# Two rows of norm roots: spread by TensorE transposes, or through device memory

## The chip, the cores and the metric

One core of one Trainium2 chip runs the whole program. The metric is the device time of one execution in microseconds (us). Engines are called TensorE (PE in the profile, PEld for its weight loads), VectorE (DVE), ScalarE (ACT), GpSimd (POOL) and SyncE (SP); "q" behind a name is the engine's own instruction sequencer, where it issues DMAs.

## The reference, cut to what matters

Two transformer-like blocks over 512 tokens (S) of width 1024 (D) in fp32. Each begins with an RMS norm and a wide projection:

```
h = x * rsqrt(mean(x*x, axis=-1) + EPS) * g      # one root r[s] for each token s
proj = h @ w_in                                  # first block: fq fk fv fg ff px pg sq sk sv sg
z    = h @ w_in_2                                # second block: c_q, c_kv, k_rope, conv gates
```

The first block then runs forgetting attention (8 heads), a multiscale pool and stick-breaking attention (4 heads), and projects back; the second runs latent attention, a short gated convolution, a projection, a feed-forward net with its own norm, and an output gate. The root r[s] depends on the token alone, so it can be applied after the projection, to its result.

## The kernel before, in words

Tokens lie in T = 4 tiles of P = 128. `x` is transposed by TensorE into `aT` (width on the partitions) and each fp32 operand is split into a high and a low part; a product is three matmuls (`three`, L545 to L547). The norm's root is not applied to `x`: it is applied when a product leaves its PSUM bank.

There are two kinds of projection. `weights_moving` leaves tokens on the partitions, so the root is a per-partition scalar, `stat[:, 3, t]`, and ScalarE applies it while it drains the bank (fq, fv, fk, sf, and lq, lkv in the second block). `weights_still` leaves the width on the partitions and the tokens along the free dimension, so VectorE needs the roots as a row of 512 that is the same on all partitions: the tile `R` ([128, 512]). Readers of `R` are `scaled` (L1971: pg, px, fg, sg), `sqk_out` (L2131), the convolution (L2267, `c` alone, with the square of the root) and, with a third row made later, the feed-forward net (L2453).

`R` is made three times in the same way. TensorE transposes `stat[:, 3, t:t+1]` broadcast to 128x128, four times, into one bank (`R1` at L728 to L732, `R2` at L1026 to L1030, `R3` in the feed-forward net; all by `turn`, L602), and VectorE copies the bank to `R` (L2023, L2257, L2443). `R1` stands on TensorE behind fk and ahead of sf; on VectorE it stands ahead of `qk_norm(T)`, the head norm of fk. `R2` stands on TensorE behind lkv and ahead of the convolution's products; on VectorE ahead of the convolution.

The order on each engine is written out by hand; semaphores tie them together. `psum_tiles` (L79) names for each PSUM tile its bank and who drains it. SyncE does little but load weight chunks of 512 KB into two raw buffers (L399), each when the split of the chunk two before it is done; GpSimd makes the high part (L464) and the low part (L472, four pieces) in one of four slots, each when TensorE has used the chunk four before it. ScalarE issues the remaining loads from its own queue, among them `g_col2` (L1467), 1024 gains of 4 bytes each, one by one.

Of the kernel before, what the change touches and what calls it, by code (L numbers as in the profile page):

```python
# [7 lines left out]
P = 128  # L8
F32 = mybir.dt.float32
# [10 lines left out]
S, D = 512, 1024  # L20
T = S // P
# [57 lines left out]
def psum_tiles():  # L79


    tiles = {}
# [12 lines left out]
    for i in range(FOX_H // 2):  # L95
        tiles["qT", i] = (4 + i, "dve", None)
    group("fk", (0, 1, 2, 3), "act", ("fk", 3))
    tiles["R1", 0] = (7, "dve", None)
    group("sf", (4, 5, 6, 7), "act", ("sf", 2))
    n = 0  # L100
    for name in ("pg", "kT", "lfT", "px", "fg", "y", "sg"):
# [19 lines left out]
        tiles["h2_last", half] = ((7, 2)[half], "dve", None)  # L121
    group("lq", (3, 1, 4, 0), "act", ("lq", 2))
    group("lkv", (5, 6, 7, 2), "act", ("lkv", 1))
    tiles["R2", 0] = (3, "dve", None)
    n = 0
    for j in range(4):
        for i, name in enumerate(("c", "xv", "b")):
# [68 lines left out]
def hybrid_kernel(nc, x_d, w_d, cols_d, pos_d, wpool_d, pt_d, gains_d, out_d):  # L196
    tiles = tile_counts(psum_tiles())
    with ExitStack() as ctx:
        def sb(name, shape, dt=F32):
            return ctx.enter_context(nc.sbuf_tensor(name, shape, dt))  # L200

        def sem(name):
            return ctx.enter_context(nc.semaphore(name))
# [15 lines left out]
        g_col2 = sb("g_col2", [P, KD])  # L219
        g_col3 = sb("g_col3", [P, KD])  # L220
        R = sb("R", [P, S])
        PT = sb("PT", [P, 2, T, S])
        sp_sum = sb("sp_sum", [P, 2, 3, P])
        neg_tri_r = sb("neg_tri_r", [P, P], F32R)
# [45 lines left out]
        def col(name, i=0, n=1):  # L270
            return cols[:, COLS[name] + i:COLS[name] + i + n]
# [49 lines left out]
        x_back = [sem(f"x_back{t}") for t in range(T)]  # L321
        out_stored = sem("out_stored")
        masks_made, ident_made = sem("masks_made"), sem("ident_made")
        w_half, r_made, R_made = sem("w_half"), sem("r_made"), sem("R_made")
        gate_scaled, gate_made = sem("gate_scaled"), sem("gate_made")
        slot_free = sem("slot_free")
        hi_made, hi_shared, w_split, w_used = sem("hi_made"), sem("hi_shared"), sem("w_split"), sem("w_used")
# [41 lines left out]
        def full(eng, key):  # L369

            kind, n = tiles[key][1]
            eng.wait_ge(tile_full if kind == "tile" else w_used, n)

        def tbank(key):
            return bank[tiles[key][0]]
# [153 lines left out]
        def _(pe):  # L529
            mm = nc.tensor.matmul  # L530

            def bank_free(key):

                before = tiles[key][2]
                if before is not None:
                    pe.wait_ge(drained[before[0]], before[1])
# [64 lines left out]
            def turn(out, in_):  # L601
                return nc.tensor.transpose(out, in_, ident[:, :])  # L602
# [122 lines left out]

            turn_heads("qT", FOX_H // 2, P, lambda t, i: qk_raw[:, t, i * P:(i + 1) * P], qk_scaled, 1)
            weights_moving([("fk", t) for t in range(T)], group4("fk"), S)
            pe.wait_ge(r_made, 1)  # L728
            bank_free(("R1", 0))
            for t in range(T):  # L730
                last = turn(tbank(("R1", 0))[:, t * P:(t + 1) * P], stat[:, 3, t:t + 1].broadcast_to([P, P]))
            last.then_inc(tile_full, 1)  # L732
            weights_moving([("sf", t) for t in range(T)],
                           [(CH["sf"], (0, 1, 2)), (CH["sf"] + 1, (3, 4, 5)), (CH["sf"] + 2, (6, 7))], SF_W)
            for i in range(2):
# [286 lines left out]
            for n in range(3):  # L1022
                lq_step(n, T - 1)
            weights_moving([("lkv", t) for t in range(T)],
                           [(CH["lkv"], (0, 1, 2, 3)), (CH["lkv"] + 1, (4, 5, 6, 7))], RANK)
            pe.wait_ge(r_made, 2)  # L1026
            bank_free(("R2", 0))
            for t in range(T):
                last = turn(tbank(("R2", 0))[:, t * P:(t + 1) * P], stat[:, 2, 4 + t:5 + t].broadcast_to([P, P]))
            last.then_inc(tile_full, 1)  # L1030
            def turn_lats():

                pe.wait_ge(lat_scaled, 1)
# [335 lines left out]
        def _(act_):  # L1369
# [18 lines left out]
            def rsqrt(at):  # L1388

                rsq[0] += 1  # L1390
                act_.wait_ge(ms_made, rsq[0])
                own(A(stat[:, 2, at], stat[:, 1, at], ACT.Ln))
                A(stat[:, 2, at], stat[:, 2, at], ACT.Exp, scale=-0.5).then_inc(rs_made, 1)
# [47 lines left out]
            def qk_rows(name, base):  # L1441
                for t in range(T):
                    if base and t == 0:
                        act_.wait_ge(tile_full, tiles["qT", FOX_H // 2 - 1][1][1])
                    full(act_, (name, t))
                    copy(qk_raw[:, t, :], tbank((name, t))[:, :], stat[:, 3, t:t + 1]).then_inc(act_step, 1)
                    steps[0] += 1
                    n = base + t
                    if n >= 2:
                        act_.wait_ge(qk_reduced, n - 1)  # L1450
                    A(sq_tmp[:, n % 2, :], tbank((name, t))[:, :], ACT.Square, scale=stat[:, 3, t:t + 1])\
                        .then_inc(qk_squared, 1)
                    act_.wait_ge(qk_squared, n + 1)
                    order[0] += 1
                    nc.scalar.sem_inc(drained["act"], 1)

            def heads_hi(name, dst, scale, made):

                for i in range(FOX_H // 2):
                    full(act_, (name, i))  # L1460
                    for n, r in enumerate((slice(0, HD), slice(HD, P))):
                        copy(dst[r, 2 * i + n, :], tbank((name, i))[r, :], scale[r]).then_inc(made, 1)

            act_.wait_ge(const_in, 48)
            act_.wait_ge(r_made, 1)
            qk_rows("fq", 0)
            act_.dma_start(g_col2[:, :], gains_d[1, 0, :].rearrange("(k p) -> p k", p=P),  # L1467
                            allow_slow_non_contiguous=True).then_inc(g_col2_in, 16)
            rsqrt(slice(16, 48))
            for t in range(T):  # L1470
                full(act_, ("fv", t))
                drain(("fv", t), copy(fv[:, t, :], tbank(("fv", t))[:, :], stat[:, 3, t:t + 1]))
            heads_hi("qT", q_parts, col("gq"), q_hi)
            qk_rows("fk", T)
            rsqrt(slice(16, 48))
            for t in range(T):
# [187 lines left out]
            squares_x2(3)  # L1664
            rsqrt(slice(4, 8))
            act_.wait_ge(r_made, 2)
            for name, dst, w, at0 in (("lq", lat_q, LQ_W, 48), ("lkv", lat_kv, RANK, 52)):
                for t in range(T):
                    full(act_, (name, t))
                    own(copy(dst[:, t, :], tbank((name, t))[:, 0:w], stat[:, 3, 4 + t:5 + t]))  # L1670
                    drain((name, t), A(PTf[:, 3072:3072 + RANK], tbank((name, t))[:, 0:RANK], ACT.Square,
                                       scale=stat[:, 3, 4 + t:5 + t], accum_out=stat[:, 0, at0 + t:at0 + t + 1]))
            rsqrt(slice(48, 56))
            for j in range(4):
                if j == 3:
                    act_.wait_ge(w_used, CH["conv"] + 12)
                    for i in range(3):
                        split_hi(aT_hi[:, 4 + i, :], y[:, i, :], col("gc", i))
                act_.wait_ge(conv_y, j + 1)
                A(sqs[:, 1, :] if j == 0 else sq2[:, j % 2, :], y[:, j, :], ACT.Square).then_inc(sq_y, 1)  # L1680
                if j == 1:
                    for i in range(4):
                        full(act_, ("latT", i))
                        split_hi(lat_parts[:, 0, i, :], tbank(("latT", i))[:, :],
                                 col("gq2", i) if i < 2 else col("gkv2", i - 2))
                    full(act_, ("krT", 0))
                    copy(k2_high[HD:QK2, 0, :], tbank(("krT", 0))[0:ROPE, :]).then_inc(k2_rope_hi, 1)
                    act_.wait_ge(k2_rope_hi, 1)
                    copy(k2_high[HD:QK2, 1:, :], k2_high[HD:QK2, 0:1, :].bitcast(F32)
                         .broadcast_to([ROPE, MLA_H - 1, S])).then_inc(k2_rope_hi, 1)  # L1690
# [191 lines left out]
        def _(dve):  # L1882
# [9 lines left out]
            def drain(key, ins):  # L1892
                order[0] += 1
                assert tiles[key][3] == ("dve", order[0]), (key, order[0])
                ins.then_inc(drained["dve"], 1)
# [83 lines left out]
            def qk_norm(base):  # L1979
                for t in range(T):  # L1980
                    n = base + t
                    dve.wait_ge(qk_squared, n + 1)
                    V.reduce_sum(stat[:, 0, 16 + 8 * t:24 + 8 * t],
                                 sq_tmp[:, n % 2, :].rearrange("p (a b) -> p a b", b=HD), axis=AX_X)\
                        .then_inc(qk_reduced, 1)
                dve.wait_ge(qk_reduced, base + T)
                rsqrt(slice(16, 48), HD)
                v = qk_raw.rearrange("p a (b c) -> p (a b) c", c=HD)
                V.tensor_tensor(v, v, stat[:, 3, 16:48].unsqueeze(2).broadcast_to([P, T * FOX_H, HD]), ALU.mult)\
                    .then_inc(qk_scaled, 1)  # L1990
# [28 lines left out]
                    V.sem_inc(drained["dve"], 1)  # L2019

            heads_lo("qT", q_parts, q_parts, col("gq"), q_hi, q_lo)
            full(dve, ("R1", 0))
            drain(("R1", 0), V.tensor_copy(R[:, :], tbank(("R1", 0))[:, :]))  # L2023
            dve.wait_ge(drained["dve"], order[0])
            qk_norm(T)

            dve.wait_ge(drained["act"], tiles["sf", T - 1][3][1])
            v0 = lf[:, 0, :].rearrange("p (t h) -> p t h", h=FOX_H)
# [224 lines left out]
            rotate(lat_q[:, :, RANK:RANK + HALF], lat_q[:, :, RANK + HALF:LQ_W], cs[:, 0, :, :], cs[:, 1, :, :], w)  # L2253
            V.sem_inc(roped, 1)

            full(dve, ("R2", 0))
            drain(("R2", 0), V.tensor_copy(R[:, :], tbank(("R2", 0))[:, :]))  # L2257
            dve.wait_ge(drained["dve"], order[0])
            own(V.memset(u[:, :, 0:KERNEL - 1], 0.0))

            def conv_lo(j):
# [349 lines left out]
```

## Time and profile before

| | |
|---|---|
| median of 3 runs | 897.89 us (897.72 to 897.96) |
| the profiled execution | 898.09 us |
| its span in the profile | 896.4 us |
| VectorE, ScalarE, GpSimd busy | 403.0, 342.9, 500.5 us |
| granted TensorE clock | 1.00 over the span |
| moved by DMA | 86.25 MB, 96 GB/s mean |

The span runs from the first to the last instruction of the profiled execution; 1.7 us of that execution's time lie outside it. A matmul's end is modelled: the starts of two in a row tell more than a duration.

### The profile page before, as it was taken

Reading aid. Unit: us, or ns where it says so; the run is one execution under the profiler, and the core shown is the slowest. Engines: PE = TensorE matmul, PEld = TensorE weight load, DVE = VectorE, ACT = ScalarE, POOL = GpSimd, SP = SyncE. Lnnn points to the kernel's source line nnn. Section 1 sums busy time; section 2 is a strip of 40 time slices with the busy share of each in tenths; the row PEclk is TensorE's granted clock in tenths of the full one; section 3 lists DMA queues with packets and bytes.
Section 4 is the critical chain, followed back from the end, with each engine's and each line's share of the span. In section 5 each row is a group of like instructions: output and inputs, shape, how many; then the busy total and the mean of one; then the engine's idle time right before and its main releaser. Section 6 shows DMA issues by size and latency. Waiting matters only on the chain.

```text
span 896.4 us, 12958 instructions
## 1 busy us (share of the span) xinstructions
PE 889.4 (99%) x4520; PEld 734.5 (82%) x4520; DVE 403.0 (45%) x699; ACT 342.9 (38%) x693; POOL 500.5 (56%) x523
## 2 busy tenths in 40 slices
PE   9999999999999999999999999999999999999998
PEld 7889887777779888887779888888888888888887
DVE  2763485678642643876667511111111112223672
ACT  4333403567725130566648532222222223233421
POOL 6988785331475877843336564444444445555453
PEclk9999999999999999999999999999999999999999
DMA  6342362212222322221213332233322322223213
GB/s 219 96 139 81 109 167 100 66 60 82 72 81 71 132 95 90 79 87 48 69 51 99 113 117 94 94 102 103 100 94 94 118 94 94 95 99 108 71 51 118
DMA packets 29725, 86.25 MB, mean 96 GB/s; under 512 B 5224, under 2 KB 8192, under 8 KB 29680
## 3 DMA queue, kind: packets, MB, share of 16 engines
q1 hardware_dynamic: 24528, 78.65, 26.3%
q10 hardware_dynamic: 5152, 6.99, 2.9%
q8 instruction: 29, 0.48, 0.2%
q14 instruction: 16, 0.13, 0.1%
HBM read 80.93 MB, written 2.10 MB: 93 GB/s over the span
## 4 chain that ended last, share of the span: by engine, by line
PE 97%; DVE 1%; POOL 1%; ACT 0%; issue 0%; POOLq 0%; ACTq 0%; DVEq 0%
PE bank L545 28%; PE bank L547 28%; PE bank L546 28%; PE bank L602 5%; PE bank L790 2%; PE bank L893 1%; POOL w_lo L472 1%; PE bank L1135 1%; PE bank L1136 1%; PE bank L885 1%; PE bank L1134 1%; PE bank L922 1%; PE bank L857 0%; PE bank L769 0%; PE bank L854 0%
## 5 line engine op out<-in xcount | busy, mean ns | idle before, releaser
L472 POOL TENSOR_TENSOR w_lo<-raw,w_hi 128x256 fp32r<-128x256 f32 (+1 forms) x420 | 409.0, 1002 | 205.6 <-ACT w_hi L1386 199.8
L545 PE MATMUL bank<-aT_hi,w_hi 128*128 128x512 f32 (+1 forms) x584 | 225.8, 387 | 0.0
L547 PE MATMUL bank<-aT_hi,w_lo 128*128 128x512 f32 (+1 forms) x584 | 222.4, 381 | 0.0
L546 PE MATMUL bank<-aT_lo,w_hi 128*128 128x512 f32 (+1 forms) x584 | 222.2, 380 | 0.0
L545 PE MATMUL bank<-w_hi,aT_hi 128*128 128x512 f32 (+3 forms) x576 | 218.5, 379 | 0.8 <-POOL w_lo L472 0.4
L547 PE MATMUL bank<-w_hi,aT_lo 128*128 128x512 f32 (+3 forms) x576 | 213.1, 370 | 0.0
L546 PE MATMUL bank<-w_lo,aT_hi 128*128 128x512 f32 (+3 forms) x576 | 212.9, 370 | 0.0
L464 POOL TENSOR_SCALAR w_hi<-raw 128x1024 fp32r<-128x1024 f32 x70 | 76.0, 1086 | 168.1 <-PE bank L547 135.6
L1386 ACT ACTIVATE w_hi<-raw 128x1024 fp32r<-128x1024 f32 x70 | 74.1, 1060 | 231.1 <-PE bank L547 214.9
L547 PEld LDWEIGHTS bank<-aT_hi,w_lo 128*128 128x128 f32 x584 | 109.8, 188 | 21.2
L545 PEld LDWEIGHTS bank<-aT_hi,w_hi 128*128 128x128 f32 x584 | 110.0, 188 | 19.9 <-issue 0.2
L546 PEld LDWEIGHTS bank<-aT_lo,w_hi 128*128 128x128 f32 x584 | 110.0, 188 | 19.6 <-issue 0.2
L545 PEld LDWEIGHTS bank<-w_hi,aT_hi 128*128 128x128 f32 x576 | 108.5, 188 | 20.0 <-issue 2.5
L547 PEld LDWEIGHTS bank<-w_hi,aT_lo 128*128 128x128 f32 x576 | 108.3, 188 | 18.5
L546 PEld LDWEIGHTS bank<-w_lo,aT_hi 128*128 128x128 f32 x576 | 108.6, 188 | 16.0
L2467 DVE TENSOR_TENSOR aT_lo<-arena,aT_hi 128x512 fp32r<-128x512 f32 x22 | 27.3, 1250 | 78.0 <-ACT aT_hi L1386 78.0
L2456 DVE TENSOR_TENSOR arena<-arena,bank 128x512 f32 (+1 forms) x22 | 15.1, 688 | 92.8 <-PE bank L547 89.8
L2453 DVE TENSOR_TENSOR arena<-bank,R 128x512 f32<-128x512 f32 x22 | 15.2, 691 | 88.3 <-PE bank L547 87.8
L1535 ACT ACTIVATE h<-bank,negmax 128x128 f32<-128x128 f32 (+1 forms) x64 | 33.9, 530 | 29.3 <-DVE negmax L2095 28.7
L2095 DVE TENSOR_REDUCE negmax<-bank 128x1 f32<-128x128 f32 (+1 forms) x64 | 31.2, 488 | 27.1 <-PE bank L769 24.9
L1386 ACT ACTIVATE arena<-bank,stat 128x512 f32<-128x512 f32 (+3 forms) x32 | 19.6, 611 | 46.2 <-PE bank L547 43.1
L1386 ACT ACTIVATE PT<-bank 128x128 f32<-128x128 f32 (+1 forms) x64 | 27.7, 436 | 12.8 <-PE bank L602 11.8
(247 smaller groups left out, 916.3 us busy)
## 6 DMA issues: line engine op xcount, KB each, us to landing
raw<-in_weights SPq DMA_DIRECT2D x141, 512.0 KB, 3.3
x<-in_x ACTq DMA_DIRECT2D x4, 512.0 KB, 5.3
y_out<-x SPq DMA_DIRECT2D x7, 256.0 KB, 4.1
x<-in_x SPq DMA_DIRECT2D x3, 512.0 KB, 8.5
g_post<-in_gains ACTq DMA_DIRECT2D x3, 512.0 KB, 3.4
k_twice<-k_twice ACTq DMA_DIRECT2D x2, 512.0 KB, 5.5
x<-in_x SPq DMA_DIRECT2D x2, 256.0 KB, 3.5
raw<-in_weights SPq DMA_DIRECT2D x2, 256.0 KB, 4.6
```

Source lines behind the costliest of these rows:

```text
L464: nc.gpsimd.tensor_scalar(w_hi[:, s, :], raw[:, r, :], 1.0, 1.0, ALU.mult, ALU.mult).then_inc(hi_made, 1)
L472: lo = nc.gpsimd.tensor_tensor(w_lo[:, s, at], raw[:, r, at], w_hi[:, s, at].bitcast(F32), ALU.subtract)
L545: mm(out, st_hi, mv_hi, start=start, stop=False)
L546: mm(out, st_hi, mv_lo, start=False, stop=False)
L547: return mm(out, st_lo, mv_hi, start=False, stop=stop)
L602: return nc.tensor.transpose(out, in_, ident[:, :])
L790: last = mm(bank[6][r0:r0 + HD, kb * P:S], v_[:, kb, i * HD:(i + 1) * HD], pt_of[i % 2][:, kb, kb * P:S], start=(kb == 0), stop=(kb == T - 1),
L1386: return A(out, in_, ACT.Copy, scale=scale)
L1535: A(P_buf[:, n % 4, 0:kw], bank[n % 3][:, 0:kw], ACT.Exp, bias=negmax[:, n % 8:n % 8 + 1], accum_out=esum[:, n % 8:n % 8 + 1]).then_inc(ex ...
L2095: V.tensor_reduce(negmax[:, n % 8:n % 8 + 1], bank[n % 3][:, 0:kw], AX_X, ALU.max, negate=True)\
L2453: V.tensor_tensor(sg_t[:, slot, :], bank[2 * slot][:, :], R[:, :], ALU.mult).then_inc(ffn_scaled, 1)
L2467: V.tensor_tensor(aT_lo[:, slot, :].unsqueeze(1), act[:, bass.ds(k, 1), :], aT_hi[:, slot, :].bitcast(F32).unsqueeze(1), ALU.subtract).the ...
```

## The change

The transposes, the two PSUM tiles `R1` and `R2` and VectorE's two copies go away; `R3` stays. In their place ScalarE issues two DMAs for each row. `roots_to_row` writes the 512 roots from `stat` ([128 partitions, 4]) to a row in device memory, each as an element of 4 bytes. `row_to_all` waits for that write and reads the row back to all 128 partitions of `R` (128 runs of 2 KB, 256 KB). VectorE waits for `R_in`.

For the first row, `roots_to_row(0)` stands ahead of the draining of fq, `row_to_all(0)` behind the high parts of q and ahead of the draining of fk; VectorE waits behind `qk_norm(T)`. For the second, `roots_to_row(1)` stands ahead of the draining of lq, `row_to_all(1)` behind the draining of lkv and its rsqrt; VectorE waits ahead of the convolution.

```diff
 psum_tiles:
-    tiles["R1", 0] = (7, "dve", None)
-    tiles["R2", 0] = (3, "dve", None)
 hybrid_kernel:
+        r_rows = nc.dram_tensor("r_rows", (2, S), F32).ap()
-        w_half, r_made, R_made = sem("w_half"), sem("r_made"), sem("R_made")
+        w_half, r_made = sem("w_half"), sem("r_made")
+        r_row_out, R_in = sem("r_row_out"), sem("R_in")
 TensorE:
             weights_moving([("fk", t) for t in range(T)], group4("fk"), S)
-            pe.wait_ge(r_made, 1)
-            bank_free(("R1", 0))
-            for t in range(T):
-                last = turn(tbank(("R1", 0))[:, t * P:(t + 1) * P], stat[:, 3, t:t + 1].broadcast_to([P, P]))
-            last.then_inc(tile_full, 1)
             weights_moving([("sf", t) for t in range(T)],
...
-            pe.wait_ge(r_made, 2)
-            bank_free(("R2", 0))
-            for t in range(T):
-                last = turn(tbank(("R2", 0))[:, t * P:(t + 1) * P], stat[:, 2, 4 + t:5 + t].broadcast_to([P, P]))
-            last.then_inc(tile_full, 1)
 ScalarE:
+            def roots_to_row(n, of):
+
+                act_.dma_start(r_rows[n, :].rearrange("(t p) -> p t", p=P), of, allow_slow_non_contiguous=True)\
+                    .then_inc(r_row_out, 16)
+
+            def row_to_all(n):
+
+                act_.wait_ge(r_row_out, n * 16 + 16)
+                act_.dma_start(R[:, :], r_rows[n:n + 1, :].broadcast_to([P, S])).then_inc(R_in, 16)
+
             act_.wait_ge(const_in, 48)
             act_.wait_ge(r_made, 1)
+            roots_to_row(0, stat[:, 3, 0:T])
             qk_rows("fq", 0)
...
             heads_hi("qT", q_parts, col("gq"), q_hi)
+            row_to_all(0)
             qk_rows("fk", T)
...
             rsqrt(slice(4, 8))
             act_.wait_ge(r_made, 2)
+            roots_to_row(1, stat[:, 2, 4:4 + T])
             for name, dst, w, at0 in (("lq", lat_q, LQ_W, 48), ("lkv", lat_kv, RANK, 52)):
...
             rsqrt(slice(48, 56))
+            row_to_all(1)
             for j in range(4):
 VectorE:
             heads_lo("qT", q_parts, q_parts, col("gq"), q_hi, q_lo)
-            full(dve, ("R1", 0))
-            drain(("R1", 0), V.tensor_copy(R[:, :], tbank(("R1", 0))[:, :]))
-            dve.wait_ge(drained["dve"], order[0])
             qk_norm(T)
+            dve.wait_ge(R_in, 16)
...
-            full(dve, ("R2", 0))
-            drain(("R2", 0), V.tensor_copy(R[:, :], tbank(("R2", 0))[:, :]))
-            dve.wait_ge(drained["dve"], order[0])
+            dve.wait_ge(R_in, 32)
             own(V.memset(u[:, :, 0:KERNEL - 1], 0.0))
```

## Rows read from the trace of the kernel before

**Rows 1.** The page, part 1: busy us, share of the span, instructions.
```profile
PE 889.4 (99%) x4520; PEld 734.5 (82%) x4520; DVE 403.0 (45%) x699; ACT 342.9 (38%) x693; POOL 500.5 (56%) x523
```
**Rows 2.** The page, part 4: the chain that ended last, by engine.
```profile
PE 97%; DVE 1%; POOL 1%; ACT 0%; issue 0%; POOLq 0%; ACTq 0%; DVEq 0%
```
**Rows 3.** Waits of PE: who for whom, us in total, times, longest.
```profile
PE bank L545 <- POOL w_lo L472: 0.4, 1, 0.4
```
**Rows 4.** The chain in order of time: start us, us, piece.
```profile
53.30 1.75 PE bank L602 x16
...
76.84 0.44 PE bank L602 x4
77.27 0.12 PE bank L545
...
294.76 0.44 PE bank L602 x4
295.20 0.23 PE bank L545
```
**Rows 5.** Timeline of PE around R2: start us, us, engine, line, operation.
```profile
294.61 0.60 PE L602 MATMUL bank<-ident,stat 128*128 128x128 f32 x4
...
294.96 0.47 PE L545 MATMUL bank<-aT_hi,w_hi 128*128 128x512 f32 x1
...
295.27 0.39 PE L546 MATMUL bank<-aT_lo,w_hi 128*128 128x512 f32 x1
```
**Rows 6.** Timeline of ACT, first block: the same columns, idle before in brackets.
```profile
27.79 0.69 ACT L1386 ACTIVATE arena<-bank,stat 128x512 f32<-128x512 f32 x1 [1.60 <-DVEq L1964]
...
33.33 0.39 ACTq L1467 DMA_DIRECT2D g_col<-in_gains  x1
...
49.25 0.69 ACT L1386 ACTIVATE arena<-bank,stat 128x512 f32<-128x512 f32 x1 [14.40 <-PE bank L547]
...
53.92 5.63 ACT L1386 ACTIVATE q_parts<-bank,cols 64x512 fp32r<-64x512 f32 x8
72.86 0.69 ACT L1386 ACTIVATE arena<-bank,stat 128x512 f32<-128x512 f32 x1 [13.30 <-PE bank L547]
```
**Rows 7.** Timeline of ACT around lkv.
```profile
290.49 0.47 ACT L1386 ACTIVATE arena<-bank,stat 128x256 f32<-128x256 f32 x1 [6.09 <-PE bank L547]
...
296.81 0.21 ACT L1393 ACTIVATE stat<-stat 128x8 f32<-128x8 f32 x1
```
**Rows 8.** Line L1467 (g_col2), its last line: issue to landing.
```profile
DMA to landing us min/median/max: 2.3/2.3/2.3
```
**Rows 9.** Line L1517: ns of an issue, min/median/max.
```profile
L1517 ACTq DMA_DIRECT2D k_low<-c_parts x8: 580/854/2067, 115.1 to 124.8; - x8
```
**Rows 10.** Busy time by stretch; the last two columns: DMA share, GB/s.
```profile
28.00:30.00 2.00, 2.00 (x10) 1.67 (x9) 0.69 (x1) 1.88 (x4) 2.00 (x4) 1.00 0.00 0
...
34.00:36.00 2.00, 2.00 (x11) 1.65 (x10) 1.37 (x4) 0.46 (x2) 1.81 (x3) 1.00 0.71 39
```
**Rows 11.** Timeline of SP: the load of the seventh chunk (c = 6).
```profile
30.54 0.33 SPq L399 DMA_DIRECT2D raw<-in_weights  x1
```
**Rows 12.** The page, part 6: KB each, median us to landing.
```profile
raw<-in_weights SPq DMA_DIRECT2D x141, 512.0 KB, 3.3
...
k_twice<-k_twice ACTq DMA_DIRECT2D x2, 512.0 KB, 5.5
```
**Rows 13.** Timeline of POOL: the two parts of that chunk.
```profile
34.40 1.05 POOL L464 TENSOR_SCALAR w_hi<-raw 128x1024 fp32r<-128x1024 f32 x1
35.53 4.92 POOL L472 TENSOR_TENSOR w_lo<-raw,w_hi 128x256 fp32r<-128x256 f32 x4
```
**Rows 14.** Timeline of DVE, both blocks.
```profile
77.31 0.69 DVE L2023 COPY R<-bank 128x512 f32<-128x512 f32 x1 [14.91 <-PE bank L602]
...
307.64 0.69 DVE L2257 COPY R<-bank 128x512 f32<-128x512 f32 x1
...
317.10 0.69 DVE L2267 TENSOR_TENSOR arena<-bank,R 128x512 f32<-128x512 f32 x1 [4.19 <-PE bank L547]
```

## The prediction

> **What bounds the kernel now.** I read the page's first part, then its chain, then TensorE's waits, then the chain in order of time around the places that the change touches. TensorE is busy 889.4 us [rows 1] of a span of 896.4 and makes 97% of the chain that ended last [rows 2]. Of its waits for other engines, the only one on the weights' supply is 0.4 us, once [rows 3]. So the time is the sum of what TensorE issues. An edit gains if it takes slots out of TensorE's order, and costs if it makes another engine late enough for TensorE to stand still; work on VectorE or ScalarE is worth nothing in itself. Both groups of transposes stand in the chain: four at 76.84, 0.44 us, and four at 294.76, 0.44 us [rows 4], with matmuls directly before and behind.
>
> **The change part by part.**
>
> *TensorE loses eight transposes.* The chain books 0.44 + 0.44 = 0.88 us [rows 4]. The starts say the same in two pieces: from the first transpose, 294.61, to the next matmul, 294.96, is 0.35 us; and that matmul's successor follows after 0.31 us, where a matmul of 512 columns takes 0.23 us in the chain, 0.08 us more [rows 4, 5]. Upper end of the gain: 0.88 us. Lower end: 2 x 0.35 = 0.70 us, if the slow first matmul is due to the change of shape from 256 to 512 columns and not to the transposes. I take 0.88, since the chain's own figure holds both pieces. What stands behind each group (sf, the convolution) simply starts earlier. TensorE also loses its waits for `r_made` and for a bank, which ended long before and are worth nothing.
>
> The trace gives 0.35 us for four transposes, 0.09 us each, before the after-effect [rows 5]. The Trainium skill, "TensorE: Matmul & The Clock Gate", section "Back-to-back issue gap", puts a sustained pair of weight load and 128-column matmul at about 81 ns; by it eight would be worth an estimated 0.65 us. The trace has the duration here and decides.
>
> *VectorE loses two copies and gains two waits.* The copies are 0.69 us each [rows 14]. The first copy waited 14.91 us for TensorE's R1 and ended at 78.00, and the norm of fk stood behind it. Its first input is two ScalarE operations of 0.69 us behind 72.86 [rows 6], so the norm can start at 74.2, 3.8 us earlier, and end up to that much earlier. TensorE wants the result only at the turning of k, behind the 96 matmuls of sf at 0.12 us and the 48 of pg at 0.23 us from 77.27 on [rows 4], near 99.8, so that is worth nothing. The second copy, at 307.64, is followed by work that waits 4.19 us for TensorE at 317.10 [rows 14]: again nothing. What is late next is in both cases TensorE's own next product.
>
> *The waits for R_in.* ScalarE issues the first read behind q's high parts, 53.92 + 5.63 = 59.55 [rows 6]. The nearest rows for its landing are 3.3 us for a weight load of twice its 256 KB, and 5.5 us, the slowest 512 KB on ScalarE's queue [rows 12]; with an issue of at most 2.1 us [rows 9] R is there between 62 and 67.2. VectorE comes to its wait behind the norm of fk, so after the 77.31 of its old copy less 3.1 us [rows 14], at 74 at the very least: a margin of 7 us. The second read is issued behind 296.81 + 0.21 [rows 7] and lands between 300.7 and 304.6; VectorE reaches it at 307.6 [rows 14], 3 us of margin at the worst bound, 7 us at the likely one. The convolution is queued behind that wait, and TensorE's banks behind the convolution; I cost both waits at 0.
>
> *ScalarE gains four issues and two waits.* The nearest row for an issue is g_col2's, 0.39 us, also a scatter of 4-byte elements; the dearest is one of L1517, 2.07 us [rows 6, 9]. The first, at 27.8, delays the draining of fq by 0.4 to 2.1 us; TensorE needs that chain at the turning of q at 53.30 [rows 4], and ScalarE idles 14.40 us before its next drain at 49.25 [rows 6]. The read at 59.6 falls into 13.30 us of idleness [rows 6], and its wait asks for a write issued 32 us earlier. The third delays the draining of lq, behind which ScalarE idles 6.09 us [rows 7]; lq's banks are wanted again only by the convolution at 295.20 [rows 4]. The fourth stands ahead of nothing until the convolution's first square, 16 us later. All four: 0, cover 6 us or more against 2.1.
>
> *The DMA engines gain two writes of 512 elements and two reads of 256 KB.* The nearest row for such a write is g_col2: 1024 elements, landed 2.3 us after its issue [rows 8], and in 34 to 36 us the engines were 71% busy moving 39 GB/s [rows 10]: small elements take engine time out of proportion. Half as many should hold them for 1 to 2.3 us. Both writes fall into stretches where the DMA share was 0.00, at 28 to 30 us [rows 10] and again at 279 to 282 us (two such rows, one shown); the next weight load after the first is issued at 30.54 [rows 11]. The reads cost at most half a weight load, 1.7 us [rows 12], on a load whose chunk TensorE wants over 10 us later: from 60 us on GpSimd waits for TensorE to free a slot, so it runs three chunks of 5.4 us ahead (24 matmuls of 0.23 us, [rows 4]). Cost 0.
>
> This is where a rule speaks against the change, and its row is the 71% for small reads [rows 10]; no row before has small writes to device memory. The Trainium skill, "DMA: Bandwidth & Descriptors", section "Specifications", says that below 512 bytes the engines do a read-modify-write. If that made the writes several times as dear as g_col2's reads, it would be the slower rival below; it leaves the sum as it is.
>
> **Sum.** -0.88 + 0 + 0 + 0 + 0 = -0.88 us. From the profiled execution: 898.09 - 0.88 = 897.21 us, of which 895.5 is span. That execution lies 0.20 us above the median of the runs, so the median should come to 897.89 - 0.88 = 897.01 us.
>
> **The rivals.**
>
> *A, the writes crowd out the seventh weight chunk (slower).* Place: the load issued at 30.54 [rows 11], landing at 33.84; GpSimd takes it at 34.40 and is done at 40.45, slowed in this stretch [rows 13]. TensorE wants it at 53.30 less 48 matmuls of 0.227 us, 42.4 [rows 4]. The margins, 0.56 and 1.95 us, make 2.5. If the write holds the engines from 28.2 for W us, the load is late by W - 2.3 and TensorE stands still for W - 4.8. At W = 5.7 the gain is used up; at W = 8, three and a half times g_col2's landing, the median is 897.01 + 3.2 = 900.2 us. For it: the engine share of small elements. Against: W of at most 2.3 by the nearest row.
>
> *B, the gain is given back.* If a later stage is bound by supply and not by TensorE, an earlier start is waited away. The only such wait is 0.4 us [rows 3], and what releases it hangs on TensorE itself. Or only the lower end, 0.70, comes. Time 897.2 to 897.8 us, within the bound.
>
> *C, the freed VectorE moves more than itself (faster).* GpSimd's 4.92 us for four pieces [rows 13] shows that VectorE can slow it by 2 us; the norm of fk now lies elsewhere against GpSimd's work. If supply were what TensorE waits for, up to 2 us would be had: 895.0 us. Against: TensorE waits 0.4 us in all for that supply.
>
> *D, R lands late.* The second wait would hold VectorE past 307.6. It needs a landing of over 10 us, and then VectorE has 4.19 us of idleness to catch up [rows 14]. Price: 0 up to a landing of 14 us, 1 us per us beyond.
>
> **How the numbers follow.** A change of under 0.2% (1.8 us) is about what a measurement of this kernel can't tell from none. Forecast (-0.88, own range 896.6 to 897.4): 0.80. B: 0.10. A: 0.05. C: 0.03. D: 0.02. Within 0.2% are the forecast, B, and the small end of A and D: 0.90. Faster is C with a small rest: 0.04. Slower is most of A and D: 0.06. The range runs from 896.1 (the forecast and 0.9 us for shifts that I have not seen) to 898.3, which takes in B and the start of A; outside lie C and most of A and D.
>
> **What would show it.** Right: TensorE's instructions fall by 8, no L602 on `stat` but the third group, a span near 895.5; the ends of fk and of lkv directly followed by sf and the convolution, the second 0.44 us and the later stages 0.88 us; no wait of VectorE on `R`; fq's drain 0.4 us later; the norm of fk 2 to 4 us earlier, the turning of k 0.44. Wrong: a TensorE wait on `w_lo` between 37 and 48 us (A), a wait of VectorE at L2267 released by the read of R (D), PE waits beyond 1 us that were not there (B), or ScalarE's issues above 2.1 us.

## The result and the profile after

The changed kernel took 900.30 us (median of 10 runs, 899.01 to 902.00); the kernel before, in runs on the same chip, 897.88 us (897.45 to 898.23). The ratio is 1.0029, with a 95% interval of 1.0020 to 1.0037: slower by 2.4 us, where 0.88 us less was forecast. That is 0.3% of the time. The runs after spread over 3 us, those before over 0.8. The profiled execution was the slowest of the ten, 902.00 us, with a span of 900.2 us against 896.4.

The page after, its first line and the first lines of parts 1 and 4, against [rows 1, 2]:

```profile
span 900.2 us, 12941 instructions
...
PE 890.8 (99%) x4512; PEld 735.7 (82%) x4512; DVE 396.0 (44%) x697; ACT 342.7 (38%) x693; POOL 498.8 (55%) x523
...
PE 93%; POOL 3%; DMA 2%; DVE 1%; issue 1%; ACT 0%; SPq 0%; POOLq 0%; DVEq 0%; ACTq 0%
```

TensorE issues eight matmuls fewer, as the change says. But its share of the chain fell from 97% to 93%, and DMA is now in the chain with 2%, GpSimd with 3%. That is more than the time lost, since the chain up to the wait now runs by way of the load and GpSimd and no longer by TensorE. "Busy" hides part of that, since a matmul at the lower clock is busy for longer. TensorE's waits, after, against [rows 3]:

```profile
PE bank L545 <- POOL w_lo L472: 2.7, 2, 2.3
```

The chain in order of time says where. After, stretches of it (start us, us, piece), against [rows 4]:

```profile
30.11 10.48 DMA raw<-in_weights
...
41.20 1.05 POOL w_hi L464
...
43.03 2.10 POOL w_lo L472 x3
...
45.18 0.79 PE bank L545
...
57.91 1.75 PE bank L602 x16
103.97 2.19 PE bank L602 x20
...
331.57 2.18 PE bank L602 x20
```

The load of the seventh weight chunk, issued at 30.11, landed 10.48 us later; such a load takes 3.3 us [rows 12]. Now the transfer that stands ahead of it, ScalarE's line L1456 in the changed kernel (the write of the roots, both of them), and L1462 (the read back): ns of the issues, and us from issue to landing.

```profile
L1456 ACTq DMA_DIRECT2D r_rows<-stat x2: 388/390/391, 28.0 to 283.4; - x2
...
DMA to landing us min/median/max: 10.6/10.7/10.8
```

```profile
L1462 ACTq DMA_DIRECT2D R<-r_rows x2: 327/336/345, 60.7 to 301.3; - x2
...
DMA to landing us min/median/max: 3.2/3.5/3.7
```

The write of 2 KB takes three times as long as a load of 512 KB. GpSimd's timeline after, against [rows 13], and SP's and TensorE's side of it:

```profile
41.20 1.05 POOL L464 TENSOR_SCALAR w_hi<-raw 128x1024 fp32r<-128x1024 f32 x1 [7.34 <-DMA raw<-in_weights]
42.34 2.78 POOL L472 TENSOR_TENSOR w_lo<-raw,w_hi 128x256 fp32r<-128x256 f32 x4
```

```profile
42.50 0.39 PE L547 MATMUL bank<-w_hi,aT_lo 128*128 128x512 f32 x1
45.18 0.79 PE L545 MATMUL bank<-w_hi,aT_hi 128*128 128x512 f32 x1 [2.29 <-POOL w_lo L472]
45.77 0.63 PE L546 MATMUL bank<-w_lo,aT_hi 128*128 128x512 f32 x1
46.20 0.63 PE L547 MATMUL bank<-w_hi,aT_lo 128*128 128x512 f32 x1
...
47.90 0.63 PE L545 MATMUL bank<-w_hi,aT_hi 128*128 128x512 f32 x1
48.33 0.47 PE L546 MATMUL bank<-w_lo,aT_hi 128*128 128x512 f32 x1
48.63 0.39 PE L547 MATMUL bank<-w_hi,aT_lo 128*128 128x512 f32 x1
```

Read the starts: 2.68 us from the last matmul before the wait to the first behind it, where 0.23 is usual, so 2.45 us are lost. Then eight steps take 3.45 us (45.18 to 48.63) in place of 1.82: the granted clock had fallen to its lower level, 1.2 GHz, at the end of the time in which TensorE stood still (1.00 from 44.8 to 45.0 us, 0.68 from 45.0 to 45.2), and came back to 2.4. Busy time by stretch shows the same; the third figure from the right is the granted clock:

```profile
42.00:44.00 2.00, 0.89 (x4) 0.39 (x3) 1.52 (x2) 0.00 (x0) 1.92 (x4) 1.00 0.00 0
44.00:46.00 2.00, 0.82 (x2) 0.73 (x3) 1.51 (x2) 0.00 (x0) 2.00 (x3) 0.77 0.00 0
46.00:48.00 2.00, 2.00 (x6) 1.51 (x6) 0.80 (x1) 0.00 (x0) 1.92 (x4) 0.50 0.76 252
```

The sum closes on landmarks that both traces have. The first is a group of eight transposes of `x` on TensorE, ahead of everything that was changed: it starts at 22.31 us in the trace of before and at 22.79 after. So this execution was 0.48 us behind before the write was issued at 28.01. The turning of q came 4.61 us later (53.30 to 57.91): these 0.48, 2.45 of waiting, 1.63 of the lower clock, and 0.05 left. The next two landmarks in the chain of before are the turnings of k and of the latents:

```profile
99.81 2.18 PE bank L602 x20
...
327.87 2.18 PE bank L602 x20
```

From the turning of q to that of k at 103.97 is 46.06 us, against 46.51 before: 0.45 less, the first group of transposes. The turning of the latents at 331.57 against 327.87 is 3.70 us late where k was 4.16 late: 0.46 less, the second group. So both gains came, each at its forecast size, and 4.1 us were paid ahead of them.

### The profile page after: what moved, and what is told of

The parts are those of the page before. It is cut to its first block, busy times and chain, and to the rows that moved or that the text cites. A ratio compares the mean times of both kernels' runs of the same rounds, so it can differ in the third digit from the quotient of the medians.

```text
span 900.2 us, 12941 instructions
## 1 busy us (share of the span) xinstructions
PE 890.8 (99%) x4512; PEld 735.7 (82%) x4512; DVE 396.0 (44%) x697; ACT 342.7 (38%) x693; POOL 498.8 (55%) x523
## 4 chain that ended last, share of the span: by engine, by line
PE 93%; POOL 3%; DMA 2%; DVE 1%; issue 1%; ACT 0%; SPq 0%; POOLq 0%; DVEq 0%; ACTq 0%
PE bank L545 27%; PE bank L547 27%; PE bank L546 27%; PE bank L602 4%; DMA raw<-in_weights 2%; PE bank L785 2%; POOL w_lo L472 2%; PE bank L888 1%; PE bank L1125 1%; PE bank L1126 1%; PE bank L880 1%; PE bank L1124 1%; PE bank L917 1%; PE bank L852 0%; PE bank L764 0%
## 5 line engine op out<-in xcount | busy, mean ns | idle before, releaser
L472 POOL TENSOR_TENSOR w_lo<-raw,w_hi 128x256 fp32r<-128x256 f32 (+1 forms) x420 | 404.7, 992 | 205.8 <-ACT w_hi L1376 200.0
L464 POOL TENSOR_SCALAR w_hi<-raw 128x1024 fp32r<-128x1024 f32 x70 | 78.6, 1123 | 173.8 <-PE bank L547 131.0
```

The source lines that it names most:

```text
L464: nc.gpsimd.tensor_scalar(w_hi[:, s, :], raw[:, r, :], 1.0, 1.0, ALU.mult, ALU.mult).then_inc(hi_made, 1)
L472: lo = nc.gpsimd.tensor_tensor(w_lo[:, s, at], raw[:, r, at], w_hi[:, s, at].bitcast(F32), ALU.subtract)
```

## The experiments

The first question was which part of the change makes the wait.

**e1, the write alone.** The kernel before, and in ScalarE's order:

```diff
             act_.wait_ge(r_made, 1)
+            roots_to_row(0, stat[:, 3, 0:T])
             qk_rows("fq", 0)
...
+            act_.wait_ge(r_row_out, 16)
             qk_rows("fk", T)
```

> The kernel before, with only the first write of 512 elements of 4 bytes added ahead of the draining of fq; both groups of transposes stay and nothing reads the row. Theory W (the write holds the DMA engines, the seventh weight chunk's load waits behind it, TensorE stands still once and comes back at the lower clock): landing of the write near 10.7 us, the load issued near 30.5 us lands near 40.6, a TensorE wait of about 2.3 us on w_lo between 42 and 45 us, and a time 4 to 5 us above before (no transposes saved), about 902. Rival S (the slower time comes from the shifted work of ScalarE and VectorE or from the reads back, and the write is hidden): within 0.3 us of before, 897.9.

Measured: 903.97 us against 898.13, ratio 1.0052 (1.0037 to 1.0068). The write landed after 11.7 us, TensorE waited 3.83 us at once where 2.3 were expected, and the clock was at the lower level behind it. Against before, the write that nobody reads costs more, 5.8 us by the medians, than the whole change did; S is out. Part of the distance is that five of e1's seven runs had the lower clock and four of the changed kernel's ten (a table further down has them); e1's two others, 900.19 and 900.73, lie 2.1 and 2.6 us above before. TensorE's wait in e1, and the stretch behind it with the granted clock third from the right:

```profile
46.46 0.79 PE L547 MATMUL bank<-w_hi,aT_hi 128*128 128x512 f32 x1 [3.83 <-POOL w_lo L474]
...
46.00:48.00 2.00, 1.54 (x4) 1.25 (x5) 0.28 (x1) 0.00 (x0) 1.92 (x3) 0.54 0.19 35
```

**e2, the second row alone.** The changed kernel with its first row made as before (the lines of the diff that concern `R1` put back, `roots_to_row(0)` and `row_to_all(0)` taken out).

> The changed kernel with its first row made by the four transposes and VectorE's copy again; only the second row goes through device memory, at the changed kernel's place. Theory W: the second write falls where GpSimd is far enough ahead, TensorE does not wait, four transposes are gone: before less 0.44 us, 897.4. Rival S (each transfer costs something of its own wherever it stands): above before by 1 us or more.

Measured: 897.89 against 898.13 us, ratio 1.0003 (0.9993 to 1.0012), by the medians 0.24 us less: too small for these runs to tell from none (0.44 were expected), and 1 us more, the least that S asks, is the interval's upper end (1.0012 is 1.1 us). The trace decides: the write landed after 10.5 us, the two loads issued from 276 to 292 us after 6.6 us (median) where 3.3 are usual, TensorE's waits were those of before, the turnings of q and k stood 46.51 us apart as before and those of k and of the latents 227.60 (99.65 to 327.25) against 228.06: 0.46 less. A write of 10.5 us is free there, though it holds loads there too.

**e3, the first write later.**

```diff
-            roots_to_row(0, stat[:, 3, 0:T])
             qk_rows("fq", 0)
...
-            row_to_all(0)
+            roots_to_row(0, stat[:, 3, 0:T])
             qk_rows("fk", T)
             rsqrt(slice(16, 48))
+            row_to_all(0)
```

> The changed kernel with the first write moved 32 us later in ScalarE's order, behind the high parts of q (near 60 us), and its read behind the draining of fk and the rsqrt (near 82 us). Same transfers, another place. Theory W: at 60 us GpSimd is three chunks ahead, so a load that is 8 us late costs TensorE nothing: before less 0.88 us, 897.0, no wait on w_lo before 100 us. Rival P (a write of 10.7 us stops TensorE wherever it falls, since loads come every 4 to 5 us): 900 or more, with a wait between 65 and 90 us.

Measured: 897.52 against 898.13 us, ratio 0.9994 (0.9985 to 1.0004); its writes landed after 9.7 and 11.2 us. No wait beyond those of before; q to k 46.06 us, k to the latents 227.62: both gains. By the medians 0.6 us less than before, where 0.9 was expected, with a sign that the interval leaves open. The three loads of 56 to 70 us landed after 6.3 us (median), 3.1 in the same stretch of before: the loads are held as well, and TensorE doesn't come to wait for them. The same transfers, 29 us later (56.89 against 28.01), cost near 3 us less than in the changed kernel: P is out, the place decides.

**e4, the same place, other runs.**

```diff
-                act_.dma_start(r_rows[n, :].rearrange("(t p) -> p t", p=P), of, allow_slow_non_contiguous=True)\
+                act_.dma_start(r_rows[n, :].rearrange("(p t) -> p t", t=T), of)\
...
-                act_.dma_start(R[:, :], r_rows[n:n + 1, :].broadcast_to([P, S])).then_inc(R_in, 16)
+                act_.dma_start(landing(n), r_rows[n:n + 1, :].broadcast_to([P, S])).then_inc(R_in, 16)
...
             dve.wait_ge(R_in, 16)
+            own(V.tensor_copy(R[:, :].rearrange("p (t a) -> p t a", t=T),
+                              landing(0).rearrange("p (a t) -> p t a", t=T)))
```

> The changed kernel with both writes as 128 runs of 16 bytes in place of 512 elements of 4 (the row lies in another order in device memory, is read into a landing tile, and VectorE's copy puts it in order: two copies of about 0.7 us, which are off TensorE's path). Same bytes, a quarter of the elements, same early place. Theory N (the landing goes by the number of elements): 2 us and a quarter of the other 8.7, so near 4.2 us, the seventh chunk in time, before less 0.88 us, 897.0. Rival H (the landing goes by the trip of a write to device memory, not by the number): still near 10.7 us, and the time of the changed kernel, 900.3.

Measured: 897.28 against 898.13 us, ratio 0.9989 (0.9979 to 0.9998): 0.85 us less, what was forecast for the change itself (the interval: 0.2 to 1.9 us less). TensorE did not wait more than before. Line L1460 in e4, the write:

```profile
L1460 ACTq DMA_DIRECT2D r_rows<-stat x2: 336/338/340, 28.9 to 278.9; - x2
...
DMA to landing us min/median/max: 1.4/2.3/3.1
```

H is out: a trip to device memory is not what takes 10.7 us. But N is not shown by it, for runs of 16 bytes differ from elements of 4 in more than number. The second question was what makes the small write dear. All further kernels but the last are the kernel before with one write in e1's place.

**e5, into on-chip memory.** Four DMAs of 128 elements in place of one of 512:

```diff
+                for t in range(T):
+                    act_.dma_start(PTf[0:1, 2608 + t * P:2608 + (t + 1) * P], of[:, t:t + 1],
+                                   allow_slow_non_contiguous=True).then_inc(r_row_out, 16)
```

> The kernel before with the same 512 elements of 4 bytes written at the same place, but into one partition of on-chip memory instead of device memory (as four DMAs of 128 elements, one behind the other on ScalarE's queue); nothing reads them. Theory M (a write of a few bytes to device memory is what is dear): landing of the last under 4 us after its issue, the seventh chunk in time, the time of before, 897.9. Theory N (each small element is dear, wherever it goes): together near 10 us, a TensorE wait near 43 us, 900 to 904.

Measured: 898.22 against 897.99 us, ratio 1.0002 (0.9992 to 1.0012). The four landed 2.0 to 3.8 us after their issues, the last of these at 31.4. M holds so far, N falls: 512 small elements as such are not dear. The four DMAs of 128 differ from one of 512 in more than the memory; e6 takes that up.

**e6, 128 bytes apart.**

```diff
+        r_rows = nc.dram_tensor("r_rows", (2, S, 32), F32).ap()
...
+                act_.dma_start(r_rows[n, :, 0].rearrange("(t p) -> p t", p=P), of, allow_slow_non_contiguous=True)\
```

> The kernel before with the first write to device memory as 512 elements of 4 bytes, but 128 bytes apart, so that no two touch the same 64 bytes; nothing reads them. Theory L (elements of one stretch of 64 bytes wait for each other, since each one's surroundings are read and written back): landing near 3 us, no TensorE wait, 897.9. Theory N (a fixed cost for each small element): near 10.7 us as before, a wait of 2 to 4 us, 900 to 904.

Measured: 897.88 against 897.99 us, ratio 1.0002 (0.9992 to 1.0012). The same 512 elements in one DMA into the same memory, and e6's line L1468 says:

```profile
DMA to landing us min/median/max: 1.9/1.9/1.9
```

**e7, half of the elements,** the first 256 of the row, close together (`stat[:, 3, 0:T // 2]` into `r_rows[n, 0:S // 2]`).

> The kernel before with half of the first write: 256 elements of 4 bytes (the roots of two of the four token tiles), nothing reads them. If the landing grows with the number of elements: 2 and half of 8.7, so near 6.3 us; the load issued near 30.5 lands some 2 us late and TensorE, with 2.5 us of margin, does not wait or waits under 0.5 us: within 0.5 us of before, 897.9. If the landing has a large fixed part: near 10 us and 900 or more.

Measured: 901.28 against 897.99 us, ratio 1.0043 (1.0028 to 1.0057). This one I expected wrongly: I still took the landing to grow with the number. It took 10.6 us for 256 elements, as for 512. With e6 it says the opposite of N: 512 elements apart are cheap, 256 close together are dear. So M in its plain form is out as well: a write to device memory is not dear in itself. Line L1468 in e7, and TensorE behind its wait:

```profile
DMA to landing us min/median/max: 10.6/10.6/10.6
```

```profile
44.49 0.50 PE L547 MATMUL bank<-w_hi,aT_hi 128*128 128x512 f32 x1 [2.25 <-POOL w_lo L474]
44.83 0.40 PE L548 MATMUL bank<-w_lo,aT_hi 128*128 128x512 f32 x1
```

**e9 to e12, the distance.** As e6 with `(2, S, n)` for n of 2, 4, 8 and 16, one execution each.

> The kernel before with the first write of 512 elements of 4 bytes, 8 bytes apart in device memory; nothing reads them. Theory C (elements that lie in one block of device memory are written one after another, and the landing goes by how many share a block): 8 in 64 bytes in place of 16, so 2 us and half of 8.7, near 6.3 us. Rival T (any neighbour in the same block costs the whole): near 10.7 us.

> The same with elements 16 bytes apart. Theory C: 4 in 64 bytes, near 4.2 us, the seventh chunk in time. Rival T: near 10.7 us and a TensorE wait near 43 us.

> The same with elements 32 bytes apart. Theory C with blocks of 64 bytes: 2 in a block, near 3 us; with blocks of 32 bytes: 1.9 us, as at 128 bytes apart. Rival T with blocks of 64 bytes: near 10.7 us.

> The same with elements 64 bytes apart. With blocks of 64 bytes or less by either theory 1.9 us, as at 128 bytes apart; above 3 us only if the block is larger.

Line L1468 in e9, e10, e11 and e12, in this order:

```profile
DMA to landing us min/median/max: 5.0/5.0/5.0
```

```profile
DMA to landing us min/median/max: 3.4/3.4/3.4
```

```profile
DMA to landing us min/median/max: 1.9/1.9/1.9
```

```profile
DMA to landing us min/median/max: 1.8/1.8/1.8
```

| bytes apart | in 32 bytes | landing us | GpSimd's wait for the seventh chunk |
|---|---|---|---|
| 4 (changed kernel, two writes) | 8 | 10.8, 10.6 | 7.34 |
| 8 | 4 | 5.0 | 3.21 |
| 16 | 2 | 3.4 | 1.43 |
| 32, 64, 128 | 1 | 1.9, 1.8, 1.9 | none |

Six writes of the first form (the changed kernel, e1, e2, e3) landed after 9.7 to 11.7 us. Theory C fits in its form, with a block of 32 bytes and not 64: from 32 bytes on nothing is left to gain, and T would have left 8 and 16 bytes at 10.7. The numbers lie near 1.9 us and 1.0 to 1.5 us more for each further element in a block. e4's runs of 16 bytes, two in 32 bytes, fit at the same place: 3.1 us there and 2.9 in e8, against 3.4 for elements 16 bytes apart. At later places such runs landed after 1.4 to 3.4 us, so the step from 16 to 32 bytes rests on this one place, with one execution for each distance. Two things are not shown. In all dear writes neighbours in device memory come from different partitions; no run writes neighbours of 4 bytes from one partition, so that may be part of the condition. And that the elements of a block wait for each other is read from the distances alone.

At 16 bytes GpSimd was late and TensorE was not. At 8 bytes the load landed after 6.34 us, 3 us late, and TensorE stood for 0.22 us more than a matmul's 0.23:

```profile
42.39 0.39 PE L549 MATMUL bank<-w_hi,aT_lo 128*128 128x512 f32 x1
42.84 0.50 PE L547 MATMUL bank<-w_hi,aT_hi 128*128 128x512 f32 x1
```

That fits the prediction's margin of 2.5 us roughly; the engines' places against each other differ from execution to execution (this load was issued at 29.73, in before at 30.54). The four kernels' times, 898.52, 898.63, 897.78 and 897.83 us, are single runs; before took 897.80.

**e8, the candidate.** e4, and the third row in the same way: `R3`, its transposes and its copy go, and on ScalarE

```diff
             for t in range(T):
+                if t == 1:
+                    act_.wait_ge(r_made, 3)
+                    roots_to_row(2, stat[:, 3, 12:12 + T])
+                if t == 3:
+                    row_to_all(2)
                 squares(emb[:, t, :], 40 + t)
```

> The candidate: all three rows through device memory, written as runs of 16 bytes, landed in a side tile and put in order by VectorE's copy; the third group of transposes leaves too (its write stands behind the first square of the embedding on ScalarE, its read behind the third). By TensorE's path: three times 0.44 us less than before, 1.32, so 896.6 where before is 897.9, and 0.4 us under the kernel with two such rows. Rival: the third row comes too late for the first rows of the feed-forward net (R is wanted near 501 us and lands near 501.5 with its copy behind it), and VectorE is late by 1 to 2 us; if that reaches TensorE, the gain of the third row is lost: 897.0 or more.

Measured: 896.59 us (11 runs, 896.23 to 897.38) against 897.99, ratio 0.9987 (0.9978 to 0.9996): 1.40 us less, 1.32 expected (the interval: 0.4 to 2.0 us less). It beats both kernels. That the third row gains on e4 is not shown by the times, 1.40 against 0.85 us less with intervals that overlap; behind the turning of the latents e8's span has 567.7 us left (894.7 - 327.04) and e4's 568.2 (895.3 - 327.11). VectorE was in fact late by 1 us against e4, 502.16 against 501.14 for its first read of `R`, and TensorE's waits behind the start of the program did not change. Rows of e8, ScalarE's fourth square of the embedding and then VectorE:

```profile
498.78 1.06 ACT L1386 ACTIVATE PT<-arena 128x1024 f32<-128x1024 f32 x1 [1.08 <-DMA r_rows<-stat]
...
500.04 0.17 DVE L1908 TENSOR_SCALAR stat<-stat 128x4 f32<-128x4 f32 x1 [5.46 <-ACT PT L1386]
...
501.51 0.62 DVE L2448 COPY R<-PT 128x512 f32<-128x512 f32 x1 [0.24 <-DMA PT<-r_rows]
502.16 0.69 DVE L2458 TENSOR_TENSOR arena<-bank,R 128x512 f32<-128x512 f32 x1
```

Most of the delay comes ahead of the read: ScalarE waited 1.08 us for the landing of the third write, with its last square behind it, and so VectorE's work on the squares began at 500.04 and not at 499.15 as in e4. The wait for the read itself is 0.24 us.

## Why the prediction was wrong

*What bounds the kernel:* right. Everything moved with what TensorE issued and with its one new wait.

*Transposes, 0.88 us:* right, 0.45 and 0.46 us between landmarks. So was the choice of the upper end. The estimate of 0.65 us from the Trainium skill ("TensorE: Matmul & The Clock Gate", section "Back-to-back issue gap") was too low by 0.26 us; the measurement decides.

*VectorE's copies and the waits for R_in, 0:* right. The reads, issued at 60.7 and 301.3, landed in 3.2 to 3.7 us, and VectorE never waited for them. But at the second place VectorE had less to spare than the 4.19 us of before [rows 14]: its operations ahead of the convolution (128x64) took 0.66 us and more each where before had 0.22 to 0.23 for most, its first read of `R` there came at 314.86 (308.50 in before, and 3.70 of that is the delay of everything), and its idle time before the next one fell to 0.76 us. TensorE did not wait for it. (The lower bound of 62 us for the first read is a slip: 59.55, an issue of 0.39 and 3.3 us make 63.2. It changes nothing.)

*ScalarE's issues, 0:* right. They took 0.39 us for a write and 0.33 to 0.35 for a read, and no chain of ScalarE reached TensorE.

*The DMA engines, 0:* this is the step that failed, and in it one term: "Half as many should hold them for 1 to 2.3 us." The write took 10.7 us. The size came from g_col2 [rows 8], which reads 1024 elements that lie close together in device memory and writes them on chip; e5 shows that a write on chip is cheap as well. The write to device memory had no row, and I bounded it from the wrong side of the memory. The second half of the step, that the DMA share of 0.00 at 28 to 30 us [rows 10] gives cover, fails with it: the cover was 2 us long, to the load at 30.54 [rows 11], and the write 10.7.

*Rival A* was the mechanism, with its place, its load and its sign (a wait on `w_lo`, 42.73 to 45.18 us), and had a chance of 0.05. Its sizes were off. With W = 10.7 its formula asks for a wait of 5.9 us; 2.45 came, and 1.63 of lower clock, which the formula left out. The load landed 1.8 us behind the write and not 3.3, so part of it may have moved meanwhile; with an issue at 30.11 and not 30.54 it landed 1.65 us before the formula's 42.24. GpSimd's split took 3.92 us (41.20 to 45.12) and not 6.05 [rows 13], 2.13 less: in before and e9 the piece of GpSimd's work that overlaps VectorE's operation on 128x2048 takes some 2 us longer, and in the changed kernel that operation ran from 36.05 to 38.34, when GpSimd was idle. TensorE came to the chunk 0.33 us later than 42.4. Against these, the 0.56 us between landing and GpSimd's start was no margin: 0.61 us lie there when GpSimd is idle too (40.59 to 41.20). 5.9 - 1.65 - 2.13 - 0.33 + 0.61 = 2.4. That A's example with W = 8 gives 900.2 us, and 900.3 was measured, is luck: neither W nor the wait was that of the example.

*The rule that spoke against the change* (the Trainium skill, "DMA: Bandwidth & Descriptors", section "Specifications": below 512 bytes the engines do a read-modify-write) named the right danger. The runs agree with it in part: the write is dear where elements share 32 bytes, 10.7 us, and not where they lie 32 bytes apart or more, 1.9 us. No run shows the engines' steps.

*Range and chances:* 896.1 to 898.3, where 900.3 came. With the cost of an operation unseen in the trace, a margin of 2.5 us, and a rule against it, 0.05 was too small.

*Why the runs after spread over 3 us:* the record has the mean granted clock of every run, and it parts them.

| kernel | mean clock 0.997 or 0.998 | 0.999 or 1.000 |
|---|---|---|
| changed | 4 runs, 901.38 to 902.00 us | 6 runs, 899.01 to 900.48 us |
| e1 | 5 runs, 903.47 to 904.43 us | 2 runs, 900.19 and 900.73 us |
| e7 | 1 run, 902.78 us | 3 runs, 900.56 to 901.32 us |

3.45 us at half the clock in a span of 900 make a mean of 0.998. The means of the two groups of the changed kernel, 901.7 and 899.9 us, lie 1.9 us apart, where the trace has 1.63. So by their clocks four of the ten runs paid near 1.63 us, the profiled one among them. The median of 900.30 lies among the others; no trace shows one of these, but e7's has such a wait at the full clock and a turning of q 2.39 us later than before (55.69), so the wait is what puts the median above before. Before less 0.91, plus the 2.45 of the one trace, would be 899.4. What decides whether a run pays is open: e7's profiled execution waited 2.25 us with the clock at 1.00 throughout, the changed kernel's 2.29. A further part of the spread is in every kernel: the first landmark, ahead of all changes, lies between 21.99 and 23.23 us in the fourteen traces.

## What to carry to other kernels

A scatter of 4-byte elements from 128 partitions into one close row of device memory held the load behind it for 7 us; give each partition's elements one run and repair the order on an engine that is idle, as e4 and e8 do. Elements 32 bytes apart land as fast, but no run here reads such a row back. Where TensorE is bound by its own issue, ask of each added DMA which load is issued next and how far ahead the supply is there: the same write was free 29 us later. And bound an unseen transfer by a row with the same kind of memory on the side that is written.

## What the runs showed that I had not expected

- The landing of 512 elements of 4 bytes in device memory: 10.7 us at 4 bytes apart, 5.0 at 8, 3.4 at 16, 1.9 at 32 and above; 256 elements at 4 bytes apart: 10.6 us.
- With the write and a load both outstanding, the profile gives the DMA engines a share of 2.39, more than there is, in one stretch, and of 0.00 in the next. Busy time after, DMA share and GB/s last:

```profile
30.00:32.00 2.00, 2.00 (x10) 1.65 (x9) 1.21 (x2) 1.88 (x4) 1.92 (x3) 1.00 2.39 33
32.00:34.00 2.00, 2.00 (x11) 1.65 (x10) 0.77 (x2) 1.76 (x3) 1.86 (x3) 1.00 0.00 0
```

  So where the share is booked is not where such a write holds the engines, and a share near zero does not say that a transfer would go through. The small load of g_col2, issued at 33.98 on ScalarE's own queue, was held as well: it landed after 8.3 us, where it took 2.3 before [rows 8].
- A TensorE wait of 2.29 us cost 1.63 us more through the granted clock in one execution, and one of 2.25 us nothing in another; by the clocks of the runs four of ten executions of the changed kernel paid.
